# Stick-breaking attention logits as two 64-row matmuls, with norms issued earlier and a tenth weight slot

## The chip, the cores and the metric

The kernel runs on all 8 NeuronCores of one Trainium2 chip. Each core works alone on two of the sixteen sequences, with the whole weights. The metric is the device time of the slowest core in microseconds (us). The median of three runs of the kernel before is 2912.78 us (2911.24 to 2913.79).

## The reference

A trunk of two layers over x (16 sequences, 2048 positions, 1024 channels), float32. Every layer is: RMS norm, a token mixer, an output projection added to the residual h, RMS norm, and a squared-ReLU MLP with 4096 hidden channels, again added to h. A final RMS norm closes it. All norms divide by sqrt(mean(h*h) + 1e-6) over the channels.

- Layer 0 projects to 2048 columns. 512 of them go through a pooling mixer (trailing mean over 2, 4, 8 or 16 positions minus the token, then a 128x128 map); the others are a gated convolution, B * conv3(C * x).
- Layer 1 projects to 2560 columns: u and v (gelu, v layer-normed and mixed within chunks of 128 positions by a causal matrix, then multiplied with u), and q, k, v of 8 heads with 64 channels each.
- Attention has no softmax. With z = q.k/8 for a head, query t and key s < t, the weight is sigmoid(z_ts) times the product over s < j < t of (1 - sigmoid(z_tj)). Its output is the weighted sum of the v of that head.

```python
z = jnp.einsum('bhqd,bhkd->bhqk', qb, kb) * scale        # 64 channels are contracted for each head
weights = where(mask, exp(log_sigmoid(z) + suffix), 0.0)
out = jnp.einsum('bhqk,bhkd->bhqd', weights, vb)
```

## The kernel before, in words

**Stages.** Channels lie on the partitions, positions along the free axis. A unit is half a sequence: 1024 positions in two tiles t = 0, 1 of 512. Twelve stages follow one another on TensorE: F (all of layer 0 for a unit), M (the input projection of layer 1 and the gating), S (the output projection and the MLP of layer 1, then the final norm). The order is F M F M S F M F M S S S, over units (sequence, half) 00 00 01 01 00 10 10 11 11 01 10 11. A join below is the passage from one stage to the next.

**Matmuls.** A group is 8 (or 16) matmuls of 128x128 by 128x512 into one of three PSUM banks (`group`, L704), all issued by the helper at L626. Each uses one weight block of 128x1024 bf16 in the ring (9 slots). The ring is filled in the order of `block_order`: from float32 weights through a GpSimd DMA the first time, and from a bf16 copy afterwards. A group is followed by its evacuation, which works on ScalarE, VectorE and GpSimd.

**Norms.** The squares of h are summed in pairs (L724, L727, L752) down to four tiles; four matmuls with ones (`ps<-X,cbs` or `ps<-ffB,cbs`, at L626) sum them over partitions; ScalarE takes Ln (L776) and Exp (L781); VectorE writes eight scaled chunks (L802 into X for the next layer, L822 as output). `norm_h` runs one such norm for a tile t. An MLP ends (`mlp`) with the output blocks c = 4 to 7, first all four for t = 0 and then all four for t = 1; eight ring slots are taken at once for it.

**Residual.** After the norm that ends an F stage each chunk of h has been spilled (`hsp<-h`) and is then reloaded for the next F or S stage by `free_h` (`h<-hsp` or `h<-xT`). `out_proj` (L1216) adds the projection to h in `evac_x` at L844.

**Attention.** It runs beside the other stages, as small items between groups (`att_item`, L1408): 320 items in all, each for 128 queries, two heads and up to 512 keys. An item is two logits matmuls (L1423), a sigmoid on ScalarE (L614, in PSUM), two scans on VectorE (L1442), a difference on GpSimd (L1456) and a transposing DMA (L1465). For four items there are 8 matmuls with V (L1479) which write 64 columns of the array each, one head into each half of PSUM. The two heads of a pair have their channels on partitions 0-63 and 64-127 of qT and kT. The logits matmuls contract all 128 rows: `spread_q` (L1398) has ScalarE copy the queries into the tile `qz` (L1404), in which the other head's rows are zero.

**Order.** The order on every engine is fixed when the program is built. A planner (`Sched`, `Machine`) holds a set of fibers, each with one pending instruction, and always emits the one that could start first by its estimated durations, shifted by a bias; conditions (`yield lambda: ...`) hold a fiber back at planning time. On the chip each engine follows its list and waits only for semaphores. A change of `mode` is priced at 0.1 us when it leaves 0 and 0.21 us otherwise.

Of the kernel before, what the change touches and what calls it, by code (L numbers as in the profile page):

```python
# [7 lines left out]
BF16 = mybir.dt.bfloat16  # L8
# [11 lines left out]
RING = 9  # L20
# [352 lines left out]
B_L0IN, B_L0OUT, B_MLP, B_V, B_U, B_VV, B_K, B_Q, B_L1OUT = 0, 16, (24, 116), 88, 92, 96, 100, 104, 108  # L373
# [3 lines left out]
def _prep_weights(inp):  # L377
# [22 lines left out]
    blocks.extend(_mov(w, 512))  # L400
    for g in range(4):
        blocks.append(_blk(w, g * 128))
    blocks.extend(_mov(w, 2048))
# [43 lines left out]
class Builder:  # L447
# [32 lines left out]
    def alloc(self):  # L480
# [35 lines left out]
        self.qz = sb("qz", [128, 1, 2, 512], BF16)  # L516
# [53 lines left out]
        self.Lqz = lst("qz", 1)  # L570
        self.Lqz0 = LT("const")
        self.p_qz = Pool(range(1))
# [59 lines left out]
    def block_order(self):  # L632
# [4 lines left out]
        for kind, s, u in self.stages:  # L637
# [4 lines left out]
            elif kind == "M":  # L642
                seq(B_V, 20)
            else:
                seq(B_L1OUT, 8)
                seq(B_MLP[1], 64)
# [57 lines left out]
    def group(self, pairs, reads, evac, fine=None):  # L704
# [4 lines left out]
        self.room += n * self.rate  # L709
        if fine is None:  # L710
            yield self.mm(self.bank(bk), pairs, reads, [self.Lbank[bk]])
        else:
            for i in range(n):
                yield self.mm(self.bank(bk), [pairs[i]], reads + [fine[i]], [self.Lbank[bk]], i == 0, i == n - 1)
# [48 lines left out]
    def rms(self, x, t, ev, power, parts=((0, 4),), bias=-0.05, slack=0.0):  # L763
# [17 lines left out]
        q = Req("act", lambda e: e.activation(out=m, in_=m, func=AF.Exp, scale=power), [], [self.Lms[ms]], 0.65)  # L781
# [55 lines left out]
    def evac_x(self, c, t, ev, gcol):  # L837
# [5 lines left out]
        def evac(bk):  # L843
            yield Req("dve", lambda e: e.tensor_tensor(out=self.h[:, c, ts], in0=self.bank(bk), in1=self.h[:, c, ts],  # L844
# [75 lines left out]
    def start_x(self):  # L920
# [9 lines left out]
        for t in range(2):  # L930
            ts = slice(t * TT, (t + 1) * TT)
            self.hcount[("F", 0, 0, t)] = 8
# [22 lines left out]
    def load_h_chunk(self, nx, c, t, cond):  # L955
# [8 lines left out]
        self.hcount[k] = self.hcount.get(k, 0) + 1  # L964
# [12 lines left out]
    def mlp(self, l, ev, then):  # L977
# [36 lines left out]
        for q in range(2):  # L1014
            if q == 0:
                yield lambda: not self.finbusy
                self.rate = 1.0
                sl = yield from self.take(8)
                for t in range(2):
                    for j in range(8):  # L1020
                        yield from w1(sl[j], j, t, j == 0)
# [7 lines left out]
            n = 8 if q == 0 else 4  # L1029
# [6 lines left out]
            if q == 1:  # L1036
                self.rate = RATE_OUT
                sl = yield from self.take(8)
                for t in range(2):
                    for c in range(4, 8):  # L1040
                        yield from w2(sl[2 * c - 8:2 * c - 6], c, t, q)
                        if t == 1:
                            self.release(sl[2 * c - 8])
                            self.release(sl[2 * c - 7])
# [50 lines left out]
    def chain_pool(self, g, t, p, seq0, tn):  # L1095
# [6 lines left out]
        def evac(bk):  # L1102
# [25 lines left out]
            if seq0:  # L1128
                yield Req("pool", lambda e: e.tensor_tensor(out=PB[:, 0:16], in0=tmp, in1=A[:, 16:32],
                                                            op=ALU.subtract),  # L1130
                          [Lt, LA], [L1], 0.2)
            b2 = yield (self.banks,)
# [11 lines left out]
    def stage_F(self, n, s, u):  # L1144
        X, LX = self.X[0], self.LX[0]
        self.mixn = [0, 0]
        self.setn = 0
# [508 lines left out]
```

How the kernel before makes its waits and increments, by code:

```python
                def body(eng):  # L192
                    for o in self.ops[engname]:
                        for d in o.waits:
                            s, v = semval(d)
                            eng.wait_ge(s, v)
                        ins = o.fn(eng)
                        if o.sig:
                            if o.dma:
                                ins.then_inc(dsem[o.chan[1]], 16)
                            else:
                                ins.then_inc(esem[engname], 1)
                    if engname == "sp":
                        for d in final_waits:
                            s, v = semval(d)
                            eng.wait_ge(s, v)
```

## Time and profile before

| | |
|---|---|
| median of 3 runs | 2912.78 us |
| profiled execution, its own time | 2921.03 us |
| span of its slowest core (core 6) | 2919.3 us |
| spans of cores 0 to 3, granted clock | 2894.6 to 2901.7 us, 0.984 to 0.985 |
| spans of cores 4 to 7, granted clock | 2912.0 to 2919.3 us, 0.977 to 0.980 |
| TensorE busy, core 6 | 2801.1 us, 96% |
| ScalarE / VectorE / GpSimd busy | 52% / 48% / 44% |
| HBM traffic | 135 GB/s over the span |

The profile is of core 6. PE is the matmul part of TensorE and PEld its weight loads; DVE is VectorE, ACT is ScalarE, POOL is GpSimd, SP is the queue that issues most DMAs. The granted clock is the share of full speed (2.4 GHz) that TensorE was given; 0.5 is its 1.2 GHz level.

### The profile page before, as it was taken

What the parts mean: (1) busy time and instruction counts of PE and PEld (TensorE: products, weight loads), DVE (VectorE), ACT (ScalarE), POOL (GpSimd) and SP (SyncE); (2) the same over time, 40 slices, a digit from 0 to 9 for tenths busy, and PEclk for the clock granted to TensorE, in tenths of its full rate; (3) what the DMA queues carried; (4) which work ended last, traced back from release to release, by engine and by line L of the source; (5) the groups of instructions that cost most, each with busy time, mean ns of one, the idle gap of its engine ahead of it and who ended that gap; (6) DMA issues with size and microseconds to landing.
All of it is one profiled execution on the core that took longest, in us unless ns stands there. A gap on an engine that the chain in (4) does not pass through costs nothing.

```text
span 2919.3 us, 43744 instructions; the slowest of 8 cores (2894.6 to 2919.3 us)
## 1 busy us (share of the span) xinstructions
PE 2801.1 (96%) x12957; PEld 1252.3 (43%) x13219; DVE 1395.3 (48%) x1706; ACT 1527.9 (52%) x2488; POOL 1286.5 (44%) x1488
## 2 busy tenths in 40 slices
PE   9999889999999999899999999999999989999998
PEld 3444334444444344344444444444444434444443
DVE  5311345454635555756656444344465665544003
ACT  3544324857338464477653475633756467545351
POOL 5432515353415666545551444340455645551113
PEclk9999999999999999999999999999999999999999
DMA  7899982445768998746775344465355485456322
GB/s 166 172 181 183 200 214 79 117 128 139 215 166 139 174 185 164 193 97 144 162 177 162 86 105 118 109 166 163 99 123 123 101 216 131 120 111 180 85 80 87
DMA packets 491478, 420.24 MB, mean 144 GB/s; under 512 B 310128, under 2 KB 334960, under 8 KB 491248
## 3 DMA queue, kind: packets, MB, share of 16 engines
q1 hardware_dynamic: 465184, 370.07, 49.7%
q0 software_dynamic: 26064, 47.36, 11.5%
q8 instruction: 113, 1.85, 0.3%
q14 instruction: 117, 0.96, 0.1%
HBM read 304.23 MB, written 89.13 MB: 135 GB/s over the span
## 4 chain that ended last, share of the span: by engine, by line
PE 88%; DMA 3%; issue 3%; DVE 2%; ACT 2%; POOL 1%; SPq 0%; DVEq 0%; ACTq 0%; POOLq 0%
PE ps L626 82%; PE ps L1423 4%; PE ps L1479 2%; DMA ring<-wblk 1%; DMA Wk<-Wq 1%; DVE vt L1269 1%; POOL ps L1116 0%; DMA stg<-xT 0%; ACT tmp L614 0%; DVE P L1442 0%; DMA oT<-stg 0%; ACT ps L614 0%; DVE X L802 0%; DVE X L752 0%; DVE h L871 0%
## 5 line engine op out<-in xcount | busy, mean ns | idle before, releaser
L626 PE MATMUL ps<-X,ring 128*128 128x512 bf16 x6016 | 1397.2, 385 | 35.1 <-DMA ring<-wblk 5.9
L626 PEld LDWEIGHTS ps<-X,ring 128*128 128x128 bf16 x6144 | 603.3, 99 | 777.9 <-issue 131.3
L1456 POOL TENSOR_TENSOR Wq<-P 128x1024 bf16<-128x1024 f32 (+2 forms) x320 | 530.2, 1659 | 590.2 <-DVE P L1442 578.9
L1442 DVE TENSOR_TENSOR_SCAN P<-ps,carry,cbs 128x512 f32<-128x512 f32 x384 | 489.1, 1279 | 381.9 <-ACT ps L614 256.8
L626 PE MATMUL ps<-mix,ring 128*128 128x512 bf16 x2752 | 654.6, 381 | 9.0 <-DMA ring<-wblk 2.8
L626 PE MATMUL ps<-ffB,ring 128*128 128x512 bf16 x2008 | 479.9, 379 | 2.1
L871 POOL TENSOR_TENSOR h<-tmp,h 128x512 f32<-128x512 f32 x220 | 287.4, 1307 | 346.1 <-DVE tmp L866 345.1
L866 DVE TENSOR_TENSOR tmp<-ps,ms 128x512 f32<-128x512 f32 x256 | 175.1, 684 | 539.4 <-PE ps L626 530.2
L614 ACT ACTIVATE tmp<-ps 128x512 f32<-128x512 f32 x512 | 303.8, 593 | 239.2 <-PE ps L626 199.0
L626 PEld LDWEIGHTS ps<-mix,ring 128*128 128x128 bf16 x2816 | 274.5, 98 | 340.8 <-issue 29.7
L614 ACT ACTIVATE ps<-ps 128x1024 f32<-128x1024 f32 (+2 forms) x320 | 280.0, 878 | 158.3 <-PE ps L1423 157.6
L626 PEld LDWEIGHTS ps<-ffB,ring 128*128 128x128 bf16 x2048 | 200.4, 98 | 241.7 <-issue 0.2
L1442 DVE TENSOR_TENSOR_SCAN P<-ps,cbs 128x128 f32<-128x128 f32 (+3 forms) x256 | 208.3, 819 | 175.9 <-ACT ps L614 129.0
L727 ACT ACTIVATE X2f<-h 128x512 f32<-128x512 f32 x128 | 80.5, 629 | 269.1 <-POOL h L871 191.8
L660 POOL DMA_DIRECT2D ring<-wblk x180 | 99.6, 555 | 233.9 <-PE ps L626 189.9
L727 ACT ACTIVATE mix<-tmp 128x512 bf16<-128x512 f32 x255 | 160.5, 630 | 30.8 <-DMA stg<-xT 5.3
L1423 PE MATMUL ps<-kT,qz 128*128 128x512 bf16 (+3 forms) x628 | 167.8, 351 | 6.8 <-DVE P L1442 5.7
L727 ACT ACTIVATE ffB<-tmp 128x512 bf16<-128x512 f32 x256 | 161.1, 629 | 24.1 <-ACT tmp L614 0.7
L844 DVE TENSOR_TENSOR h<-ps,h 128x512 f32<-128x512 f32 x128 | 88.0, 688 | 157.6 <-PE ps L626 155.2
L852 ACT ACTIVATE X<-h,cfs 128x512 bf16<-128x512 f32 x128 | 92.0, 719 | 71.5 <-DVE h L844 70.9
L626 PE MATMUL ps<-ring,X 128*128 128x512 bf16 x498 | 115.9, 388 | 10.0 <-DVE vt L1269 6.7
L752 POOL TENSOR_TENSOR ffB<-ffBf 128x512 bf16<-128x512 f32 x64 | 81.9, 1285 | 72.5 <-ACT ffBf L727 70.7
(83 smaller groups left out, 1644.2 us busy)
## 6 DMA issues: line engine op xcount, KB each, us to landing
ring<-wbf SPq DMA_DIRECT2D x540, 256.0 KB, 2.9
ring<-wblk POOLq DMA_DIRECT2D x180, 256.0 KB, 7.0
wbf<-ring SPq DMA_DIRECT2D x180, 256.0 KB, 6.3
stg<-xT SPq DMA_DIRECT2D x96, 256.0 KB, 5.0
h<-xT SPq DMA_DIRECT2D x64, 256.0 KB, 8.4
hsp<-h SPq DMA_DIRECT2D x64, 256.0 KB, 4.7
h<-hsp SPq DMA_DIRECT2D x64, 256.0 KB, 7.7
oT<-mixf SPq DMA_DIRECT2D x32, 256.0 KB, 7.4
```

The costliest lines, as they stand in the source:

```text
L614: q = Req("act", lambda e: e.activation(out=out, in_=in_, func=func, **kw), reads, writes, dur, bias=bias)
L626: ins = pe.matmul(out, lhsT=l, rhs=r, start=(first and i == 0), stop=(last and i == n - 1), skip_group_check=True)
L660: (lambda slot, b, src: lambda e: e.dma_start(out=self.ring[:, slot, :], in_=src[b]))(slot, b, src),
L727: a = Req("act", lambda e: e.activation(out=out, in_=in_, func=AF.Square), reads, writes, 0.63, bias=bias)
L752: q = Req(eng, lambda e: e.tensor_tensor(out=X[:, SQ[i][2], t * TT:(t + 1) * TT].rearrange("p (a n) -> p a n", a=2), in0=Xf[:, SQ[i][0], h ...
L844: yield Req("dve", lambda e: e.tensor_tensor(out=self.h[:, c, ts], in0=self.bank(bk), in1=self.h[:, c, ts], op=ALU.add), [], [self.Lbank[b ...
L852: yield self.any_of(d, Req("act", lambda e: e.activation(out=X[:, c, ts], in_=self.h[:, c, ts], func=AF.Copy, scale=g), [self.Lh[c][t], se ...
L866: yield Req("dve", lambda e: e.tensor_tensor(out=self.tmp[:, b, :], in0=self.bank(bk), in1=self.ms[:, r2, :], op=ALU.mult), [self.Lms[r2]] ...
L871: q = Req(eng, lambda e: e.tensor_tensor(out=self.h[:, c, ts], in0=self.tmp[:, b, :], in1=self.h[:, c, ts], op=ALU.add), [self.Ltmp[b]], [ ...
L1423: ins = pe.matmul(zt[:, h * 512:h * 512 + w], lhsT=qz[:, h, r * 128:(r + 1) * 128], rhs=self.kT[:, a, k0:k0 + w], start=True, stop=True, s ...
L1442: yield Req("dve", (lambda h: lambda e: e.tensor_tensor_scan(out=P[:, h, 0:w][:, ::-1], data0=zt[:, h * 512:h * 512 + w][:, ::-1], data1=l ...
L1456: yield Req("pool", lambda e: e.tensor_tensor(out=W4, in0=P[:, :, 1:w + 1].rearrange("p h (j n) -> p h j n", n=128), in1=P[:, :, 0:w].rear ...
```

## The change

The logits matmuls contract 64 rows each: the first head's from partitions 0-63 of qT and kT, the second's from 64-127, into two PSUM banks. The tile `qz`, its memsets and its copies go. The memory that it took becomes a tenth ring slot. The planner prices such an item as `mode=1`.

In the norms, `norm_h` of both tiles is spawned before the MLP of an F stage with a bias of -2, and the Exp gets a bias of -2. M stages begin with the four u blocks, and a first group may take its input chunk by chunk (`ok`). Blocks are taken from the ring one by one where eight or four were taken. In an F stage the wait for the final norm of the stage before (`finbusy`) moves behind three of the four groups. `hcount` becomes a set: `out_proj` no longer waits for all eight chunks of h, and `evac_x` waits for its own. The reload of h in an M stage is spread over groups 16 to 31 of that stage (`mg`).

```diff
@@ -17,7 +17,8 @@
 EPS = 1e-6
-RING = 9
+TAILC = 4
+RING = 10
 RATE_IN = 0.4
@@ -370,7 +371,7 @@
-B_L0IN, B_L0OUT, B_MLP, B_V, B_U, B_VV, B_K, B_Q, B_L1OUT = 0, 16, (24, 116), 88, 92, 96, 100, 104, 108
+B_L0IN, B_L0OUT, B_MLP, B_V, B_U, B_VV, B_K, B_Q, B_L1OUT = 0, 16, (24, 116), 92, 88, 96, 100, 104, 108
 NBLK = 180
@@ -397,9 +398,9 @@
     w = inp["cd_w_in"][0]
-    blocks.extend(_mov(w, 512))
     for g in range(4):
         blocks.append(_blk(w, g * 128))
+    blocks.extend(_mov(w, 512))
     blocks.extend(_mov(w, 2048))
@@ -513,7 +514,6 @@
         self.ao = sb("ao", [128, 2, 512], BF16)
-        self.qz = sb("qz", [128, 1, 2, 512], BF16)
         o0 = self.off
@@ -567,9 +567,6 @@
         self.Lao = lst("ao", 2)
-        self.Lqz = lst("qz", 1)
-        self.Lqz0 = LT("const")
-        self.p_qz = Pool(range(1))
         self.LCY, self.LCC = lst("cy", 3), lst("cc", 3)
@@ -640,7 +637,7 @@
             elif kind == "M":
-                seq(B_V, 20)
+                seq(B_U, 20)
             else:
@@ -701,16 +698,19 @@
-    def group(self, pairs, reads, evac, fine=None):
+    def group(self, pairs, reads, evac, fine=None, ok=None):
...
         self.room += n * self.rate
+        self.mg += self.inm
         if fine is None:
...
             for i in range(n):
+                if ok is not None:
+                    yield ok(i)
                 yield self.mm(self.bank(bk), [pairs[i]], reads + [fine[i]], [self.Lbank[bk]], i == 0, i == n - 1)
@@ -778,7 +778,7 @@
         self.banks.free(bk)
-        q = Req("act", lambda e: e.activation(out=m, in_=m, func=AF.Exp, scale=power), [], [self.Lms[ms]], 0.65)
+        q = Req("act", lambda e: e.activation(out=m, in_=m, func=AF.Exp, scale=power), [], [self.Lms[ms]], 0.65, bias=-2)
         q.tab = AF.Ln
@@ -834,13 +834,14 @@
-    def evac_x(self, c, t, ev, gcol):
+    def evac_x(self, c, t, ev, gcol, hk):
...
         def evac(bk):
+            yield lambda: c in self.hcount.get(hk, ())
             yield Req("dve", lambda e: e.tensor_tensor(out=self.h[:, c, ts], in0=self.bank(bk), in1=self.h[:, c, ts],
@@ -929,7 +930,7 @@
             ts = slice(t * TT, (t + 1) * TT)
-            self.hcount[("F", 0, 0, t)] = 8
+            self.hcount[("F", 0, 0, t)] = set(range(8))
             ev = Ev()
@@ -961,7 +962,7 @@
         k = (kind, s, u, t)
-        self.hcount[k] = self.hcount.get(k, 0) + 1
+        self.hcount.setdefault(k, set()).add(c)
@@ -1015,9 +1016,11 @@
                 self.rate = 1.0
-                sl = yield from self.take(8)
+                sl = []
                 for t in range(2):
                     for j in range(8):
+                        if t == 0:
+                            sl += yield from self.take(1)
                         yield from w1(sl[j], j, t, j == 0)
@@ -1026,7 +1029,7 @@
                 self.release(sl[0])
-            n = 8 if q == 0 else 4
+            n = 8 if q == 0 else 8 - TAILC
             for c in range(n):
@@ -1035,13 +1038,15 @@
                 self.rate = RATE_OUT
-                sl = yield from self.take(8)
+                sl = []
                 for t in range(2):
-                    for c in range(4, 8):
-                        yield from w2(sl[2 * c - 8:2 * c - 6], c, t, q)
+                    for c in range(8 - TAILC, 8):
+                        if t == 0:
+                            sl += yield from self.take(2)
+                        yield from w2(sl[2 * (c + TAILC) - 16:2 * (c + TAILC) - 14], c, t, q)
                         if t == 1:
-                            self.release(sl[2 * c - 8])
-                            self.release(sl[2 * c - 7])
+                            self.release(sl[2 * (c + TAILC) - 16])
+                            self.release(sl[2 * (c + TAILC) - 15])
             self.ffgen += 1
@@ -1129,6 +1134,7 @@
                           [Lt, LA], [L1], 0.2)
+            yield lambda: t not in self.finbusy
             b2 = yield (self.banks,)
@@ -1145,6 +1151,7 @@
         self.setn = 0
+        self.mg = 0
         yield lambda: self.vbusy == 0 and self.cdone == 2
@@ -1154,12 +1161,11 @@
             if i not in blk:
-                blk[i] = [] if n == 0 else (yield from self.take(4))
+                blk[i] = []
             sl = blk[i]
...
             seq0 = u == 0 and t == 0
-            yield lambda: t not in self.finbusy
             if i == 0:
@@ -1175,8 +1181,10 @@
             for b in (1, 2, 0, 3):
+                if b == 3:
+                    yield lambda: t not in self.finbusy
                 fine = n == 0 and i == 0 and b == 1
-                if n == 0 and t == 0:
+                if t == 0:
                     sl += yield from self.take(1)
@@ -1204,34 +1212,36 @@
             return f
-        yield from self.mlp(0, ev2, then)
-
         def dst(t):
...
                 yield from f(c, *a)
-                self.free_h(nx, c, t, lambda: (c, t) in spilled)
+                nd2.add((c, t))
+                self.free_h(nx, c, t, lambda: (c, t) in spilled and self.mg >= 16 + 1 * (t * 8 + c))
             return g
         for t in range(2):
-            self.M.spawn(self.norm_h(ev2[t], t, 16, dst(t), nd2), -0.2)
+            self.M.spawn(self.norm_h(ev2[t], t, 16, dst(t), nd2), -2)
+        yield from self.mlp(0, ev2, then)
     def out_proj(self, kind, s, u, src, Lsrc, gcol):
-        sl = yield from self.take(8)
+        sl = []
         evo = [Ev(), Ev()]
...
             ts = slice(t * TT, (t + 1) * TT)
-            yield lambda: (self.mixn[t] == 8 if kind == "F" else (s, u, t) in self.mready) and \
-                self.hcount.get((kind, s, u, t)) == 8
+            yield lambda: (self.mixn[t] == 8 if kind == "F" else (s, u, t) in self.mready)
+            hk = (kind, s, u, t)
             if t == 1:
...
             for c in range(8):
+                if t == 0:
+                    sl += yield from self.take(1)
                 yield from self.group(self.wpairs(sl[c], src, ts), [self.Lring[sl[c]]] + [Lsrc[k][t] for k in range(8)],
-                                      self.evac_x(c, t, evo[t], gcol))
+                                      self.evac_x(c, t, evo[t], gcol, hk))
                 if t == 1:
@@ -1289,13 +1299,14 @@
         self.cn = [0, 0]
+        self.inm = 1
         self.use_scratch("sgu")
...
         self.qkn = 0
-        sl = yield from self.take(8)
+        su, sl = [], []
@@ -1313,7 +1324,6 @@
             ts = slice(t * TT, (t + 1) * TT)
-            yield lambda: t in self.nd3
             Lx = [LX[k][t] for k in range(8)]
@@ -1321,10 +1331,14 @@
                     self.un[t] += 1
-                yield from self.group(self.wpairs(sl[4 + g], X, ts), [self.Lring[sl[4 + g]]] + ([] if g == 0 else Lx), evac,
-                                      fine=Lx if g == 0 else None)
+                if t == 0:
+                    su += yield from self.take(1)
+                yield from self.group(self.wpairs(su[g], X, ts), [self.Lring[su[g]]] + ([] if g == 0 else Lx), evac,
+                                      fine=Lx if g == 0 else None, ok=lambda k: lambda: (k, t) in self.nd3)
                 if t == 1:
-                    self.release(sl[4 + g])
+                    self.release(su[g])
+            if t == 0:
+                sl = yield from self.take(4)
             for n in range(4):
@@ -1355,6 +1369,7 @@
                 self.release(sl[0])
+        self.inm = 0
         self.M.spawn(self.attention(s, u), 0.4)
@@ -1368,7 +1383,7 @@
                 nch = u * 2 + tq + 1
-                st = dict(left=nch, nch=nch)
+                st = dict(left=nch)
                 prev = [None] * 4
@@ -1378,9 +1393,6 @@
         yield lambda: self.qkn == 24
-        for a in range(4):
-            for tq in range(2):
-                self.M.spawn(self.spread_q(a, tq, items), 0.0)
         tot = float(sum(x["w"] for x in items))
@@ -1395,22 +1407,10 @@
-    def spread_q(self, a, tq, items):
-
-        z = yield self.p_qz
-        ts = slice(tq * TT, (tq + 1) * TT)
-        for h in range(2):
-            hp = slice(h * 64, (h + 1) * 64)
-            yield Req("act", (lambda h, hp: lambda e: e.activation(out=self.qz[hp, z, h, :], in_=self.qT[hp, a, ts], func=AF.Copy))(h, hp),
-                      [self.LqT[a][tq], self.Lqz0], [self.Lqz[z]], 0.64)
-        mine = [x["g"]["st"] for x in items if x["g"]["a"] == a and x["g"]["tq"] == tq]
-        mine[0]["z"] = z
-
     def att_item(self, s, u, x):
...
         a, c, first, end, tq, st = G["a"], G["c"], G["first"], G["end"], G["tq"], G["st"]
-        yield lambda: "z" in st
-        qz, Lqz = self.qz[:, st["z"]], self.Lqz[st["z"]]
+        il = tq * 4 + r
         zs = yield self.zsets
@@ -1420,13 +1420,11 @@
             for h in range(2):
-                ins = pe.matmul(zt[:, h * 512:h * 512 + w], lhsT=qz[:, h, r * 128:(r + 1) * 128],
-                                rhs=self.kT[:, a, k0:k0 + w], start=True, stop=True, skip_group_check=True)
+                hp = slice(h * 64, (h + 1) * 64)
+                ins = pe.matmul(zt[:, h * 512:h * 512 + w], lhsT=self.qT[hp, a, il * 128:(il + 1) * 128],
+                                rhs=self.kT[hp, a, k0:k0 + w], start=True, stop=True, skip_group_check=True)
             return ins
-        yield Req("pe", zmm, [Lqz, self.LkT[a][c]], Lz, w / 1200.0 + 0.01, bias=-0.04, wslack=0.5)
-        st["zn"] = st.get("zn", 0) + 1
-        if st["zn"] == 4 * st["nch"]:
-            self.p_qz.free(st["z"])
+        yield Req("pe", zmm, [self.LqT[a][tq], self.LkT[a][c]], Lz, w / 2400.0 + 0.07, bias=-0.04, wslack=0.5, mode=1)
         z3 = zt[:].rearrange("p (h n) -> p h n", h=2)[:, :, 0:w]
@@ -1539,9 +1537,6 @@
         yield Req("dve", lambda e: e.memset(self.cb[:, 128:640], 0.0), [], [self.Lz0], 0.3)
-        for h in range(2):
-            yield Req("pool", (lambda h: lambda e: e.memset(self.qz[(1 - h) * 64:(2 - h) * 64, :, h, :], 0.0))(h), [],
-                      [self.Lqz0], 0.8)
         yield self.dma(self.cf[:], self.cf_d, [], [self.Lcf], "cf", kb=72.0)
@@ -1601,6 +1596,8 @@
         self.main_t = 0
+        self.inm = 0
+        self.mg = 0
         self.r2 = {}
```

## Rows read from the trace of the kernel before

**Rows 1.** The page: busy time and share of each engine.

```profile
PE 2801.1 (96%) x12957; PEld 1252.3 (43%) x13219; DVE 1395.3 (48%) x1706; ACT 1527.9 (52%) x2488; POOL 1286.5 (44%) x1488
```

**Rows 2.** Waits of PE: us in total, times, longest us.

```profile
PE ps L626 <- DVE X L752: 28.2, 11, 3.9
...
PE ps L626 <- DVE vt L1269: 6.7, 8, 1.2
```

**Rows 3.** Stretches at the joins: length, PE busy (matmuls), clock, DMA share, GB/s.

```profile
353.00:371.00 18.00, 10.93 (x41) 0.76 1.04 216
786.00:804.00 18.00, 13.52 (x51) 0.91 0.90 252
1541.00:1559.00 18.00, 14.69 (x52) 0.81 0.92 258
1963.00:1981.00 18.00, 13.20 (x46) 0.81 0.79 224
...
1162.00:1202.00 40.00, 28.66 (x118) 0.87 0.87 217
2337.00:2369.00 32.00, 23.34 (x95) 0.87 1.11 247
2640.00:2669.00 29.00, 24.23 (x96) 0.88 1.02 289
```

**Rows 4.** Timeline of PE at an F to M join: start, us, instructions.

```profile
787.85 1.03 PE L626 MATMUL ps<-X,cbs 128*128 128x512 bf16 x4
791.34 1.02 PE L626 MATMUL ps<-X,cbs 128*128 128x512 bf16 x4 [2.46 <-DVE X L752]
792.67 0.38 PE L626 MATMUL ps<-X,ring 128*128 128x512 bf16 x1 [0.30 <-DVE X L802]
...
796.64 3.53 PE L626 MATMUL ps<-X,ring 128*128 128x512 bf16 x8 [0.29 <-DVE X L802]
```

**Rows 5.** The same join, other engines in the timeline.

```profile
791.11 10.68 DVE L802 SCALAR_TENSOR_TENSOR X<-h,cfs,ms 128x512 bf16<-128x512 f32 x16
...
791.94 10.68 SPq L619 DMA_DIRECT2D h<-hsp  x16
```

**Rows 6.** Timeline at the S to F join.

```profile
1166.09 0.69 ACT L776 ACTIVATE ms<-ps,cfs 128x512 f32<-128x512 f32 x1
...
1172.84 0.63 ACT L781 ACTIVATE ms<-ms 128x512 f32<-128x512 f32 x1
...
1174.76 0.73 DVE L822 SCALAR_TENSOR_TENSOR mixf<-h,cfs,ms 128x512 f32<-128x512 f32 x1
```

**Rows 7.** Timeline at an S to S join: a reload of h.

```profile
2347.55 0.44 SPq L619 DMA_DIRECT2D h<-hsp  x1
```

**Rows 8.** PE groups of L1423 by shape: count, busy us, mean ns, idle before.

```profile
L1423 PE MATMUL ps<-kT,qz 128*128 128x512 bf16 x436 | 132.3, 385 | 6.7 <-DVE P L1442 5.7 <-issue 0.6
...
L1423 PE MATMUL ps<-kT,qz 128*128 128x384 bf16 x64 | 15.6, 326 | 0.1
L1423 PE MATMUL ps<-kT,qz 128*128 128x256 bf16 x64 | 12.5, 277 | 0.0
...
L1423 PE MATMUL ps<-kT,qz 128*128 128x128 bf16 x64 | 9.0, 223 | 0.0
```

**Rows 9.** Timeline of PE within F 01, attention bursts between groups.

```profile
738.94 0.59 PE L1423 MATMUL ps<-kT,qz 128*128 128x512 bf16 x2
739.37 1.89 PE L626 MATMUL ps<-mix,ring 128*128 128x512 bf16 x8
...
774.68 1.89 PE L626 MATMUL ps<-ffB,ring 128*128 128x512 bf16 x8
776.50 1.05 PE L1479 MATMUL ps<-Wk,V 128*64 128x512 bf16 x8
777.48 1.90 PE L626 MATMUL ps<-mix,ring 128*128 128x512 bf16 x7
```

**Rows 10.** ACT group that fills the padded tile.

```profile
L1404 ACT ACTIVATE qz<-qT 64x512 bf16<-64x512 bf16 x64 | 39.8, 622 | 31.7 <-PE ps L1423 30.1
```

## The prediction

> **What bounds the kernel now.** I read the page first. TensorE is busy 2801.1 of 2919.3 us and every other engine about half of that [rows 1], so time goes only where TensorE waits, runs at a lower clock, or streams columns that it need not. The waits of PE come next: the largest item by far is 28.2 us in 11 waits, and it is the norm matmul waiting for the last pair sum (DVE X L752) [rows 2]. All waits of that view add to some 91 us. They sit at the joins, so I made a table of the joins by stretches [rows 3]. Full-array matmuls of 512 columns follow one another every 0.216 us (739.37 plus eight of them is the next start in the timeline). Length less count times 0.216 is what a stretch loses, to waits and to the clock together; a few records can be missing, so it is rather an upper value. The four F to M joins, in order: 18 - 41 x 0.216 = 9.1, then 7.0, 6.8 and 8.1 us, together 31.0. The S to F join loses 40 - 118 x 0.216 = 14.5, and the two S to S joins 11.5 and 8.3, together 34.3. The mean clock in these stretches is 0.76 to 0.91: after each wait TensorE is granted its 1.2 GHz level for a few microseconds, and the next matmuls take double.
>
> **Early norms, u blocks first, first group by chunks.** At the F to M join at 787 us the norm matmuls of t = 0 are the first thing PE does after the last output group, at 787.85 [rows 4], though the sums for t = 0 were complete long before: four groups of 16 matmuls for t = 1 (13.8 us) had run in between. So ScalarE and VectorE make X of t = 0 only then; VectorE writes 16 chunks in 10.68 us, 0.67 each [rows 5], and PE follows it one matmul at a time, until its first group is through at 796.86 [rows 4]. Moved into the 13.8 us, the chain of t = 0 is: evacuation and add about 2, square and pair sum 1.3, norm matmuls 0.9, Ln and Exp 1.4, eight chunks 5.3, so about 11 us. VectorE is otherwise used for about 1.4 of each 3.45 us there, which hides it. PE can then begin M at 787.71 with u groups. The old path spent 9.15 us up to 796.86 for 1.7 us of norms and 1.7 of group: 5.7 us are waits, and 1.2 GHz behind them costs about 1.5 more. What is late next is the norm of t = 1: its sums still come 3 us after the last group, as 791.34 shows [rows 4]. Eight groups of t = 0 (13.8 us) lie before its first use, but PE meets the norm matmuls in program order, and the planner has so far placed them 2.5 to 3.9 us too early. I leave 1.7 us per join for that: 31.0 - 4 x 1.7 = 24 us gained. Bounds: 0 (the waits only move) and 31. The gating phase behind it keeps its waits for VectorE (vt L1269, 6.7 us in 8 waits [rows 2]); eight chunks of X for t = 1 fall into it as before.
>
> **Exp with a bias, finbusy behind three groups.** In the S to F join Ln ended at 1166.78 and its Exp began only at 1172.84, with other work and table loads between them; the first output chunk started at 1174.76 [rows 6]. With the bias that is up to 6 us sooner. F may also start its first three groups (5.2 us) before the final norm is out, which covers the 3.9 us wait, the longest in [rows 2], and with it the fall to 1.2 GHz. Of 14.5 us I take 9, with bounds 0 and 14.5. The waits for chains of the convolution and pooling behind it remain.
>
> **hcount by chunk, out_proj one block at a time.** In an S to S join the projection could start during the wait for the norm of t = 1. But h of the new stage is still being reloaded as the final norm gives chunks free, at 2347.55 for one of them [rows 7], and with three PSUM banks PE gets at most three groups ahead of it; the norm needs a bank too. Of 19.8 us I take 4, bounds -6 (the banks are held and the norm is later) and 19.8.
>
> **Spread reload, tenth slot, single takes.** Sixteen loads of h were issued in 10.68 us right at the join [rows 5], where the DMA share is 0.79 to 1.04 [rows 3]. Moved behind group 16 they fall beside value and key groups, which read nothing of h, and have over 20 groups (35 us) before `out_proj`. A gain only where PE waits for ring blocks, mainly in the first join: nothing taken beyond the 24, bounds -2 and 5. Nothing else of the ring is on the path.
>
> **Logits over 64 rows.** 640 matmuls: 448 of 512 columns and 64 each of 384, 256 and 128 (640 in all, of which [rows 8] have 628 recorded) are 278,528 columns, 116.1 us at 2.4 GHz, and 0.0025 us each on top. If two halves stream together, half goes: 58.8 us. That they may is seen only in the sibling, L1479: eight matmuls of 512 columns, each on half of the columns of the array, take 777.48 - 776.50 = 0.98 us [rows 9], where one after the other would be 1.73. But there PE also pays for changing: the group before it (774.68 plus 8 x 0.216 = 776.41) ends 0.09 before the burst begins, and of the 0.98 us four pairs explain 0.86, so about 0.1 goes at each end. The padded logits pay nothing of that: 738.94 to 739.37 is 0.43 for two, as full-array matmuls do [rows 9]. In the PE timeline of core 6 the logits form 305 bursts; 263 are entered from a full-array matmul and 301 left to one (the rest stand beside a burst of L1479, which has changed already). 564 changes x 0.096 = 54 us. So the item is 58.8 - 54 = 5 us gained: 20 ns won on an item of 512 columns, 140 ns lost on one of 128. Bounds of a change: 0, and the 0.17 us by which a matmul (0.385 mean, [rows 8]) outlasts its slot of 0.216 plus a weight load of about 0.1, together 0.26 us. The latter makes 147 us, a loss of 88; the former a gain of 59. I take 0.096 as the nearest row.
>
> The Trainium skill, TensorEngine Tiling (Array Packing), section Key Properties, says that changing the tiling mode, not just the tile, drains TensorE. The trace agrees for column halves with about 0.1 us at each end [rows 9]; no run here shows it yet for row halves. By the page's Theoretical Speedup table alone (2x for a dimension of at most 64) the edit would bring the 58.8 us; the drain rule takes most of it back.
>
> **Copies into qz.** 64 ScalarE copies, 39.8 us, go [rows 10]. ScalarE is at 52% and is not what PE waits for; 0 taken, bounds 0 and 4.
>
> **Sum.** 24 + 9 + 4 + 5 = 42 us against the profiled execution's 2921.03: 2879. That execution stands 8.2 us above the median of the runs shown, so in the measure of the runs 2912.8 - 42 = 2871 us.
>
> **Rivals.**
> 1. *Changes of mode cost more than they do for column halves, and decide.* With 37 us from the joins and 58.8 from the columns, the kernel gets slower once a change costs over 95.8 / 564 = 0.17 us. For it: the planner prices leaving at 0.21 and adds 0.07 to each item, 0.38 per item together; a 128-column weight load into the row half may stand open, where L1479 loads 64 columns. Against it: the same planner overprices L1479 (0.15 + 4 x 0.216 + 0.31 = 1.32, measured 1.07). At 0.20 us: 113 - 58.8 = 54 lost, 37 won, 2930 us; at 0.26 us 2964.
> 2. *The joins give nothing back.* The early norm matmuls are put in front of output groups before their sums are ready, as the S joins show already, VectorE is late in the gating phase instead, and attention with its plan prices lands elsewhere. For it: every wait in the first row of [rows 2] is a place where the plan was too early. Against it: 13.8 us of cover for t = 0. Then only the 5 us of the logits are left, less a little: 2910 us.
> 3. *Row halves change for nothing* and joins gain as forecast: 59 + 37, 2817 us. For it: the weights of a row half can be loaded without touching the other. Against it: both ends of every L1479 burst.
>
> **How the numbers follow.** Forecast (gain of 18 to 65 us) 0.60, rival 1 0.17, rival 2 0.15, rival 3 0.08. This kernel's measurement can tell about 0.2% (6 us) from no change. Faster: 0.60 + 0.08 + a third of rival 2 = 0.73. Same: half of rival 2 and a little of rival 1, 0.09. Slower: 0.18. The forecast's own range is 2848 to 2895; for 8 in 10 I go to 2838 below, where more of the 65 us at the joins comes back, and to 2924 above, which takes in rival 2 and the near part of rival 1.
>
> **What would show it.** Early norms: in the F to M stretches `ps<-X,cbs` for t = 0 stands among the `ps<-mix,ring` groups, no one-matmul rows wait for L802, and the row DVE X L752 falls from 28 to below 15 us. Exp follows Ln within 1 us. Logits: L1423 appears as 64x512 with two starts a few ns apart and the next group 0.31 us later, 0.1 us of it the change; if the next group comes 0.4 us after, rival 1 holds, and if 0.22, rival 3. DVE vt L1269 well over 10 us would speak for rival 2. The forecast is wrong if the whole count of PE's waits stays near 90 us, or if the two starts of a pair are 0.2 us apart.

## The result: 30 us faster where 42 were forecast

Median 2883.38 us against 2913.28 us before; the ratio is 0.9888 (95% interval 0.9863 to 0.9914). The forecast was 2871. On two other chips the kernel before ran at 2896 to 2898 us. As the cores of a die run at a lower granted clock in some executions, this text uses a steadier number beside each ratio: the mean span of all cores on dies whose granted clock was at least 0.985 (rounded), over all runs of a kernel. For the kernel before it is 2888.1, 2888.2 and 2888.4 us, each measured anew on one of these two chips; for the changed kernel, on one of them, 2858.9, so 29.3 less.

In the profiled execution after, TensorE is busy 2793.9 of 2881.5 us on the slowest core (core 4). The waits of PE there (us in total, times, longest):

```profile
PE ps L623 <- DVE h L845: 11.6, 7, 3.2
...
PE ps L623 <- DVE vt L1279: 8.2, 8, 1.7
PE ps L623 <- DVE X L752: 7.8, 2, 4.5
PE ps L623 <- DMA mix<-dsp: 7.8, 1, 7.8
```

The wait for the norm's sums fell from 28.2 us to 7.8 as forecast [rows 2], but two waits stand in its place: for the reload of h in the projection (DVE h L845) and, once, for the mixer outputs (mix<-dsp). Stretches of the same length at the same joins (length, PE busy and matmuls, then the other engines, clock, DMA share, GB/s):

```profile
343.00:361.00 18.00, 16.43 (x66) 6.96 (x67) 12.55 (x19) 3.77 (x6) 7.50 (x10) 0.86 1.02 194
772.00:790.00 18.00, 18.00 (x85) 8.17 (x84) 10.50 (x16) 11.39 (x16) 2.39 (x2) 1.00 0.37 117
...
1939.00:1957.00 18.00, 18.00 (x82) 7.99 (x81) 9.72 (x14) 11.20 (x16) 2.54 (x2) 0.96 0.33 109
1161.00:1201.00 40.00, 29.89 (x122) 11.33 (x121) 29.67 (x38) 17.03 (x27) 18.96 (x31) 0.87 0.97 266
2306.00:2338.00 32.00, 24.05 (x107) 9.56 (x106) 25.24 (x30) 18.80 (x29) 12.19 (x10) 0.95 1.07 245
2609.00:2638.00 29.00, 25.74 (x100) 10.49 (x99) 15.77 (x22) 16.16 (x28) 6.34 (x5) 0.85 1.00 296
```

By length less count times 0.216 the F to M stretches lose 3.7, 0, 0 and 0.3 us, where they lost 31.0 [rows 3]. (The third has 85 matmuls like the second.) The first stretch begins inside a wait of PE from 340.07 to 344.57, and 2.9 us of it lie before 343: with these it loses 6.7. Three of these joins have no wait left. The S joins lose 13.6, 8.9 and 7.4 where they lost 34.3 in all: 4.4 gained, where 9 + 4 = 13 were forecast. The timeline of PE at the join which [rows 4] show before:

```profile
774.31 7.07 PE L623 MATMUL ps<-X,ring 128*128 128x512 bf16 x32
781.22 1.03 PE L623 MATMUL ps<-X,cbs 128*128 128x512 bf16 x4
782.08 7.07 PE L623 MATMUL ps<-ring,X 128*128 128x512 bf16 x32
```

The u groups start straight after the last output group, and the norm of t = 1 comes after four of them. The logits by shape (count, busy us, mean ns), and a pair in the timeline:

```profile
L1424 PE MATMUL ps<-kT,qT 64*128 64x512 bf16 x448 | 87.4, 389 | 4.4 <-DVE P L1440 4.4
...
L1424 PE MATMUL ps<-kT,qT 64*128 64x128 bf16 x64 | 7.4, 227 | 0.0
```

```profile
2303.44 1.89 PE L623 MATMUL ps<-ffB,ring 128*128 128x512 bf16 x8
2305.26 0.39 PE L1424 MATMUL ps<-kT,qT 64*128 64x512 bf16 x2
2305.58 5.35 PE L623 MATMUL ps<-X,ring 128*128 128x512 bf16 x24
```

Eight matmuls after 2303.44 end at 2305.17, so 0.09 us are lost on entering. The two logits matmuls and the way out take 0.32 us. In [rows 9] the padded pair took 0.43 and no more. Busy time of the logits, all four shapes, fell from 169 us [rows 8] to 114.5, but busy time leaves out the changes of mode.

### The profile page after: what moved, and what is told of

It reads as the page before. It is cut to its first block, busy times and chain, and to the rows that moved or that the text cites. A ratio compares the mean times of both kernels' runs of the same rounds, so it can differ in the third digit from the quotient of the medians.

```text
span 2881.5 us, 43787 instructions; the slowest of 8 cores (2851.7 to 2881.5 us)
## 1 busy us (share of the span) xinstructions
PE 2793.9 (97%) x13215; PEld 1197.7 (42%) x13215; DVE 1390.7 (48%) x1704; ACT 1481.5 (51%) x2418; POOL 1287.4 (45%) x1488
## 3 DMA queue, kind: packets, MB, share of 16 engines
q0 software_dynamic: 26064, 47.36, 11.6%
## 4 chain that ended last, share of the span: by engine, by line
PE 83%; DMA 6%; DVE 3%; POOL 3%; issue 3%; SPq 1%; ACT 1%; DVEq 0%; POOLq 0%; ACTq 0%
PE ps L623 79%; PE ps L1424 3%; PE ps L1477 2%; DVE P L1440 2%; DMA ring<-wblk 1%; DMA stg<-xT 1%; POOL Wq L1454 1%; SPq L616 1%; POOL h L872 1%; DMA Wk<-Wq 1%; DMA h<-xT 1%; POOL ps L1121 1%; DMA h<-hsp 1%; DVE vt L1279 1%; DMA mix<-dsp 1%
## 5 line engine op out<-in xcount | busy, mean ns | idle before, releaser
L623 PEld LDWEIGHTS ps<-X,ring 128*128 128x128 bf16 x6144 | 586.9, 98 | 769.6 <-issue 125.0
L623 PE MATMUL ps<-mix,ring 128*128 128x512 bf16 x2816 | 662.0, 382 | 12.3 <-DMA mix<-dsp 7.8
L623 PEld LDWEIGHTS ps<-mix,ring 128*128 128x128 bf16 x2816 | 265.5, 98 | 348.2 <-issue 52.4
L845 DVE TENSOR_TENSOR h<-ps,h 128x512 f32<-128x512 f32 x128 | 87.7, 686 | 133.0 <-PE ps L623 125.3
L1424 PE MATMUL ps<-kT,qT 64*128 64x512 bf16 (+3 forms) x640 | 113.2, 356 | 9.4 <-DVE P L1440 9.3
L752 POOL TENSOR_TENSOR ffB<-ffBf 128x512 bf16<-128x512 f32 x64 | 81.0, 1271 | 85.1 <-ACT ffBf L727 83.2
```

The lines of the kernel that those rows point to most:

```text
L623: ins = pe.matmul(out, lhsT=l, rhs=r, start=(first and i == 0), stop=(last and i == n - 1), skip_group_check=True)
L752: q = Req(eng, lambda e: e.tensor_tensor(out=X[:, SQ[i][2], t * TT:(t + 1) * TT].rearrange("p (a n) -> p a n", a=2), in0=Xf[:, SQ[i][0], h ...
L1424: ins = pe.matmul(zt[:, h * 512:h * 512 + w], lhsT=self.qT[hp, a, il * 128:(il + 1) * 128], rhs=self.kT[hp, a, k0:k0 + w], start=True, sto ...
```

## The experiments

The changed kernel again and eleven variants, each timed beside the kernel before. "Mean" is the number defined above. "Waits" is the sum of all distances between starts of PE that exceed 0.75 us, less 0.216 each, on the mean core: the average over the eight cores of the profiled execution. "1.2 GHz" is half the time in which PE streamed at that level, again on the mean core.

| kernel | ratio to before | mean, us | waits | 1.2 GHz |
|---|---|---|---|---|
| before | 1 | 2888.2 | 82.3 | 20.3 |
| changed, again | 0.9903 (0.9870-0.9937) | 2858.9 | 69.2 | 11.4 |
| e1 joins, padded logits | 0.9911 (0.9878-0.9944) | 2858.1 | 63.5 | 12.0 |
| e2 64-row logits alone | 1.0050 (1.0004-1.0095) | 2887.9 | 85.5 | 25.4 |
| e9 as e1, same order, 64 rows | 0.9897 (0.9841-0.9954) | 2859.3 | 70.0 | 12.8 |
| e3 nine slots | 0.9923 (0.9892-0.9955) | 2861.7 | 67.7 | 15.5 |
| e5 late norms | 0.9943 (0.9920-0.9966) | 2872.1 | 73.3 | 17.1 |
| e8 reload not spread | 0.9942 (0.9916-0.9968) | 2869.2 | 75.1 | 17.7 |
| e7 wait for all of h | 0.9915 (0.9884-0.9946) | 2862.8 | 69.7 | 14.3 |
| e6 Exp without bias | 0.9895 (0.9859-0.9930) | 2860.5 | 71.1 | 10.2 |
| e4 measured prices | 0.9916 (0.9890-0.9942) | 2860.8 | 70.7 | 16.8 |
| e10 padded price | 0.9845 (0.9786-0.9903) | 2849.8 | 62.1 | 13.0 |
| e11 e10, early reload | 0.9878 (0.9838-0.9918) | 2849.8 | 62.1 | 11.3 |

The scatter from die to die gives each mean a standard error of 0.4 to 2.0 us. So a difference below 3 us between two of these kernels is not resolved. Variants e1 to e4 ran on one chip, the others and the changed kernel on another; the kernel before gives 2888.1 and 2888.2 us there. The waits and the 1.2 GHz cost of the kernel before are from the first chip.

**The changed kernel again** (no edit).

> The changed kernel itself, as the yardstick for the kernels of this comparison. Its trace waits 71 us on the mean core and lost 15 us at the 1.2 GHz level when it was first taken; the same is expected here, and a ratio to before of 0.989 to 0.993.

As expected: 69.2 us of waits against 70.8 the first time. The 1.2 GHz level cost 11.4 us against 15.2.

**e1: joins with the padded logits.**

```diff
-lhsT=self.qT[hp, a, il * 128:(il + 1) * 128], rhs=self.kT[hp, a, k0:k0 + w]
+lhsT=qz[:, h, r * 128:(r + 1) * 128], rhs=self.kT[:, a, k0:k0 + w]
...
-RING = 10
+RING = 9
```

> The changed kernel with the joins as they are, but logits over the zero-padded query tile again, as before the change (ScalarE copies included), and nine ring slots. Theory A (a change between full array and row halves costs about 0.1 us at each end, so the logits edit is worth some 5 us; the joins carry the rest): 2888 us against 2883, at most 2893; no step of 0.1 us around L1424 pairs, two logits matmuls of 512 columns take 0.43 us again. Rival B (the 64-row logits also draw less current, and the fall of the time at 13/16 of the clock, 158 to 200 us before and 67 to 69 us after on cores 4 to 7, is theirs): the 13/16 time on cores 4 to 7 is back at 150 us or more and the time is 2900 or more. Rival C (the padded tile is as good or better when the joins are right): 2878 or less.

2858.1: within 1 us of the changed kernel, so neither theory A's 5 us nor a gain of rival C's size. The joins carry the whole gain that shows; the logits edit, the tenth slot and the copies together add nothing that does. No core of the profiled execution had any time at a granted clock of 13/16 (0.81), a third level that the records show beside full speed and 0.5; that is no verdict on rival B, since the changed kernel had none either when it was run again.

**e2: the logits edit alone**, on the kernel before.

> The kernel before with one part of the change: logits over 64 rows, priced as in the change, without the padded tile; nine ring slots, joins as before. Theory A: about 5 us faster than before, 2908 (2902 to 2914), with 0.1 us at each end of a pair. Rival B (less current): 2895 or less, with the 13/16 time on cores 4 to 7 under 100 us. Rival C (the plan prices of the items shift attention so that more waits arise): slower than before by 5 us or more.

2887.9 against 2888.1: nothing, where theory A expected 5 us. Rival B falls: two cores of the profiled execution spent 161 us each at 13/16, as the kernel before does at times. The stream of matmuls got 5 us shorter than in the profile before, of which the logits with their changes are about 2, and the cost of the 1.2 GHz level, most of it behind the joins, grew by 5 us (25.4 against 20.3).

**e9: the same order, only the operands differ.** The instruction lists of e1 and e9 are equal on all five engines.

```diff
 # e1, with spread_q, qz and its prices kept
-lhsT=qz[:, h, r * 128:(r + 1) * 128], rhs=self.kT[:, a, k0:k0 + w]
+lhsT=self.qT[hp, a, il * 128:(il + 1) * 128], rhs=self.kT[hp, a, k0:k0 + w]
```

> The joins kernel with the padded tile, planned exactly so (the same instructions in the same order on every engine, the copies into qz and nine ring slots included), only that the logits matmuls read qT and kT over 64 rows. So it is the price of the 64-row form alone. Theory A (0.1 us at each end, two halves at once): the logits take 1 to 5 us less of PE than padded, waits and the 1.2 GHz share stay at the padded kernel's 64 and 12 us, ratio to before 0.990, within 4 us of the padded kernel. Rival (the form itself disturbs: weights of a half array load in the open, or the clock falls more often because half of the rows work): the time at 1.2 GHz is above 18 us or waits are above 70, and the ratio is that of the changed kernel or worse.

With waits over 0.75 us counted as one slot of 0.216, the logits with their changes take 119.7 us of the mean core in e9 and 122.1 in e1: the form by itself is worth 2.4 us. The whole differs by 1.2 the other way, within the noise, with waits of 70.0 against 63.5 us in the same order, on different chips; so two profiled executions can differ by 6 us in their waits with no cause in the order. The 1.2 GHz level costs 12.8 us against 12.0, so the rival's clock part falls; its limit of 70 us for the waits was met only by that noise.

**e3: nine slots.**

```diff
-RING = 10
+RING = 9
```

> The changed kernel with nine ring slots in place of ten, nothing else. Theory A (the ring is not on the path; PE waits 6.3 us for ring blocks after the change against 8.7 before): within 4 us of 2883. Rival: the tenth slot carries a part of the gain in the first pass over the weights, then 2888 to 2895 and PE waits for DMA ring<-wblk of 12 us or more.

2861.7, 2.8 us slower. The time is inside theory A's 4 us, and just inside the noise. But PE waits 13 to 17 us for `ring<-wblk` on four of the eight cores (0, 1, 3, 5), as the rival said, against 4 to 9 in the changed kernel. The tenth slot is worth a little at most, and it is the padded tile's memory.

**e5: late norms.**

```diff
-        for t in range(2):
-            self.M.spawn(self.norm_h(ev2[t], t, 16, dst(t), nd2), -2)
         yield from self.mlp(0, ev2, then)
+        for t in range(2):
+            self.M.spawn(self.norm_h(ev2[t], t, 16, dst(t), nd2), -0.2)
```

> The changed kernel with the norms of an F stage spawned after its MLP with the old bias, as before the change; all other parts stay. Theory A (early norms take 24 us at the four F to M joins): 18 to 28 us slower than the changed kernel, with ps<-X,cbs for t = 0 behind the last output group again and one-matmul rows that wait for X L802. Rival (the wait only moves into the gating phase): slower by less than 8 us.

2872.1, 13.2 us slower: below the 18 to 28 of theory A, far above the 8 of the rival. Its join (timeline of PE) is again as before, one matmul behind each chunk:

```profile
772.72 0.59 PE L623 MATMUL ps<-X,ring 128*128 128x512 bf16 x1 [2.51 <-DVE X L802]
...
777.30 0.38 PE L623 MATMUL ps<-X,ring 128*128 128x512 bf16 x1 [0.29 <-DVE X L802]
```

Where the early norms gain and where they lose shows on the mean core, as waits plus the 1.2 GHz cost (an F to M join here is the 46 us before the first gating matmul of the M stage, the stage behind it lasts to 15 us after the last one, and the M 01 to S 00 join is the 55 us after that):

| place | before | changed, again | e5 | e8 |
|---|---|---|---|---|
| first F to M join | 10.1 | 5.3 | 6.8 | 10.3 |
| M stage behind it | 8.8 | 1.8 | 1.9 | 11.0 |
| other three F to M joins | 14.8 | 0 | 14.6 | 2.8 |
| M 01 to S 00 join | 0 | 9.1 | 2.8 | 0 |

In three joins, undoing the early norms brings back all that was lost there before; in the first they are worth 1.5 us; and 6.3 us go again at the M 01 to S 00 join, where the wait for the mixer outputs is 2.4 us in e5 and 7.3 in the changed kernel. That an M stage which starts earlier reaches these loads before they have landed is the explanation that fits; no run moves the loads alone.

**e8: the reload not spread.**

```diff
-self.free_h(nx, c, t, lambda: (c, t) in spilled and self.mg >= 16 + 1 * (t * 8 + c))
+self.free_h(nx, c, t, lambda: (c, t) in spilled)
```

> The changed kernel without the spread of the h reload: each chunk is reloaded as soon as it is normed and spilled. Theory A (a new wait of 7 to 9 us at the join from M 01 to S 00 comes from the spread: 16 reloads of h run just when the mixer outputs are loaded, with the float32 weights of the first pass beside them): that wait falls from 7.8 to 3 us or less, and the kernel is 0 to 6 us faster than the changed one. Rival (the wait comes from the shorter M stage alone): the wait stays at 7 us or more.

The wait for mix<-dsp is gone, as theory A said, but the kernel is 10.3 us slower, not faster. At the first F to M join the eight reloads for t = 0 are now issued among the output groups, and the float32 blocks that PE needs next are late (timeline of SP and of PE, core 1):

```profile
338.99 7.20 SPq L616 DMA_DIRECT2D h<-xT  x8
...
360.80 8.75 PE L623 MATMUL ps<-ring,X 128*128 128x512 bf16 x32 [6.12 <-DMA ring<-wblk]
```

Between 335 and 362 us on core 4 such a block took 14.4 us from issue to landing, in the changed kernel 8.3 (`--dma` of both runs):

```profile
ring<-wblk POOLq DMA_DIRECT2D x8, 256.0 KB, 14.4
```

The first join and the M stage behind it wait 15.7 us on the mean core in e8, 6.0 in the changed kernel. By releaser, small waits included, the wait for `ring<-wblk` rose by 3.9 us (4.9 against 1.0), and the gating phase's wait for VectorE by 5.6 (vt L1279 and vn L1265, 7.7 against 2.1). So the late blocks are shown, but they are less than half of it. This is the step that the prediction counted at nothing.

**e7: all eight chunks of h awaited.**

```diff
             hk = (kind, s, u, t)
+            yield lambda: len(self.hcount.get(hk, ())) == 8
```

> The changed kernel, but the output projection waits again (when planned) until all eight chunks of h for its tile have their reload issued, as before the change. Theory A (in an S stage PE only gets three groups ahead of the reload of h, so going by chunk is worth little): within 3 us of the changed kernel; the waits for DVE h L845 (11.6 us) fall and a wait for the norm (X L752) of about as much returns. Rival (by chunk is worth the 4 us taken in the prediction or more): 4 us slower or more.

3.9 us slower: the 4 us of the prediction, not the "within 3" of the expectation. The two S to S joins lose 20.6 us on the mean core, waits and 1.2 GHz cost together, against 15.9. DVE h L845 leaves the longest waits, X L752 is at 14.5 on the slowest core (11.4 in the changed kernel again).

**e6: Exp without its bias.**

```diff
-[], [self.Lms[ms]], 0.65, bias=-2)
+[], [self.Lms[ms]], 0.65)
```

> The changed kernel without the bias of -2 on the Exp of a norm. Theory A (the Exp used to come up to 6 us after its Ln, and the norm at the S to F join with it): the S1 to F join (11.7 us of waits in the changed kernel) grows by 3 to 6 us, the whole is 4 to 8 us slower than the changed kernel. Rival: another engine hides it and the time stays within 3 us.

1.6 us slower, within the rival's 3 and within the noise. Around the S to F join (from 35 us before the first pooling matmul to 30 behind it) the mean core waits 11.5 us against 10.7, not the 3 to 6 more of theory A.

**e4 and e10: the planner's prices.** e4 sets each change to 0.1 us, the pair to `w / 2400.0 + 0.01` and the burst with V to 0.03 on top of its columns. e10 (the end of the line):

```diff
-w / 2400.0 + 0.07, bias=-0.04, wslack=0.5, mode=1)
+w / 1200.0 + 0.01, bias=-0.04, wslack=0.5)
```

> The changed kernel, with the planner's prices set to what the trace shows: 0.1 us for each change of mode (0.1 and 0.21 before), 0.01 us on top of the columns for a logits pair (0.07 before), 0.03 for the burst with V (0.15 before). Nothing of the computation changes, only the order. Theory A (the plan runs late by 0.2 us per item, 70 us in the whole, so that PE comes to evacuations too early): PE's waits fall from 74 to 60 us or less and the time to 2872. Rival (the plan's slack on PE does not matter, the joins are planned by other engines' times): within 5 us of 2883.

> The changed kernel (64 rows, no padded tile, ten ring slots), but the planner prices a logits pair as it priced the padded one: columns / 1200 plus 0.01 us, no change of mode. Theory A (what the changed kernel lost against the joins with padded logits comes from the plan: with 0.38 us on each item the plan runs up to 0.2 us late per item): waits of 66 us or less on the mean core and 5 to 12 us faster than the changed kernel. Rival (the plan's price does not matter, each order has its own luck at the joins): waits of 68 to 75 us and within 4 us of the changed kernel.

e4 is 1.9 us slower, which is noise, e10 9.1 us faster than the changed kernel, which is not. True prices bring nothing, so my reason for the gain of e10 (a plan that runs late) does not hold. The waits of e10 are 7 us fewer, 4.4 of them in the middle of S 00 (3.0 against 7.4). Whether that is a property of the price or the luck of one order, these runs don't tell.

**e11: e10 with the reload over groups 2 to 17.**

```diff
-self.mg >= 16 + 1 * (t * 8 + c)
+self.mg >= 2 + 1 * (t * 8 + c)
```

> A version that might beat both: 64 rows, ten slots, the logits pair priced as columns / 1200 plus 0.01 us without change of mode, and the reload of h spread over groups 2 to 17 of an M stage in place of 16 to 31. Theory A: the loads are over before the mixer outputs are loaded, so the 7.3 us wait at the join from M 01 to S 00 goes to 3 us or less and the kernel gains 3 to 6 us over the one with that price alone (2849.8 us on the mean undisturbed core). Rival: the early loads hold up the norm of t = 1 or the ring, and it is within 2 us of that or slower.

The wait for mix<-dsp is gone (0 against 7.3 us), and the first M stage waits 7.4 us instead of 1.8: nothing gained, as the rival said, but not for its reason. On all eight cores the M stage waits for VectorE's gating work, not for a DMA (PE ps L1273 <- DVE vn L1265, 5.2 to 6.2 us; before the change 4.6 on the mean core). Before it, in the join, the wait for `ring<-wblk` is 1.9 us against 1.0. With e8 this shows that the mixer wait needs the reloads beside it. What their earlier place costs is a wait for VectorE, and why VectorE is later there stays open.

## Why the prediction was right in direction and too large

**Logits: right mechanism, 5 us forecast, 2 measured.** The two starts of a pair lie 3 ns apart in the timeline, so the halves stream together. Entering costs 0.096 us more than a full-array follower; leaving costs 0.103, not 0.096. With 271 entries and 302 exits in the timeline of core 0 that is 57.1 us against the 58.8 saved: 1.7 us, and 2.4 between e1 and e9. Neither is resolved in the time of the kernel. Rival 1 (0.17 us and more) and rival 3 (nothing) are out.

The Trainium skill (TensorEngine Tiling (Array Packing), Key Properties) says that a change of tiling mode drains TensorE. For row halves the trace now agrees, with about 0.1 us at each end; the page's 2x (Theoretical Speedup) holds for the stream alone.

**Early norms: right in the joins, too large in the whole.** I took 24 us for the early norms, the u blocks first and the first group by chunks together. The four joins gave just that: 31.0 went to 4.0, or to 7.0 with the part of the wait before 343. But the term stands in the sum as if nothing behind the joins would change, and there it was mis-sized: undoing the norms alone (e5) costs only 13.2. No run undoes the u blocks or the chunks; with late norms (e5) they leave three joins at 14.6 us of 14.8, so by themselves they bring nothing there. Two things take the difference. PE meets the norm of t = 0 too early in the first join, among the output groups (timeline of PE, core 4):

```profile
344.57 1.86 PE L623 MATMUL ps<-X,cbs 128*128 128x512 bf16 x4 [4.50 <-DVE X L752]
```

This is rival 2's mechanism, in one join of four. (Rival 2's other sign, the row of vt in the gating phase well over 10 us, did not come: 8.2.) And behind M 01 stands a new wait, for the mixer outputs. PE asks for them 17 us after the issue of the first (833.05), where it was 20 before (851.95 to 872.24). There the changed kernel issues one load in 5.1 us, with five reloads of h and the float32 blocks in the same stretch; the dsp loads take 14.2 us to land in the median (12.1 before), and PE waits 7.8 us. The queue of SP, and the issues between 826 and 858 us with their time to landing:

```profile
833.05 5.11 SPq L616 DMA_DIRECT2D mix<-dsp  x1
```

```profile
ring<-wblk POOLq DMA_DIRECT2D x8, 256.0 KB, 9.3
...
mix<-dsp SPq DMA_DIRECT2D x8, 128.0 KB, 14.2
```

Both are needed for it: later norms (e5) bring the wait from 7.3 to 2.4 us on the mean core, reloads elsewhere (e8, e11) to 0.

**Exp and finbusy: 9 us forecast, 1 to 4 us gained.** Exp does follow Ln at once, at 1170.13 where Ln began at 1169.35 and took 0.69; before, 6.1 us lay between them [rows 6]. F starts before the final norm is out. But PE then waits for the evacuation of a gated convolution, `mix L1091` (timeline of PE and of VectorE at the S to F join):

```profile
1178.67 0.69 DVE L1130 SCALAR_TENSOR_TENSOR pb<-ps,pa 128x512 bf16<-128x512 f32 x1 [2.80 <-POOL rtmp L1127]
...
1179.94 0.68 DVE L1091 TENSOR_TENSOR mix<-ps,cy 128x512 bf16<-128x512 f32 x1
...
1180.77 3.35 PE L623 MATMUL ps<-X,ring 128*128 128x512 bf16 x8 [4.25 <-DVE mix L1091]
```

A wait of 3.9 us went and one of 4.3 came: 14.5 us lost became 13.6 on the slowest cores. On the mean core, between the bounds given for e6, waits and 1.2 GHz cost went from 17.4 to 13.7 (14.4 in the first profile). The new wait is not for what `finbusy` guards. Its group had ended by 1176.5, but VectorE first stood 2.8 us before the pooling's `pb`, for GpSimd, and wrote one output chunk; only then came L1091. That order is the plan's; no run changes it. The bias by itself is not resolved (e6).

**By chunk: 4 us forecast, 3.9 measured** (e7), with the cause that both texts name: PE now waits for h L845 (11.6 us) where it waited for the norm.

**Spread reload and slot: 0 forecast, 10.3 and 2.8 measured** (e8, e3; the latter within the noise). The prediction's bound of 5 was wrong. It saw the DMA share of 1.04 at the first join [rows 3] but put no price on it. With early norms eight loads of 256 KB stand before the float32 blocks that PE needs next, and the gating phase behind them is later too (e8). The latter part, the larger, is seen but not explained.

Two readings in the prediction are slightly off and change nothing: the waits of PE in that view add to 93 us, not 91, and M could begin at 787.85 [rows 4], not 787.71.

**The sum.** Undoing one part at a time gives 13.2 + 10.3 + 3.9 + 2.8 + 1.6 = 31.8, and the logits 0 to 2, against 29.3 for the whole. That the parts add up so nearly is no proof that they are independent: the mixer wait needs two of them. The u blocks first, the first group by chunks, the single takes and the moved `finbusy` were not undone. By account, from before to the changed kernel again, the mean core's waits fell by 13.1 us, the cost of the 1.2 GHz level by 8.9, and the remaining stream by 3.7 (the single-matmul gaps of 0.3 us and the logits). That the total lies inside the forecast's range is in part luck: the reload, counted at 0, made up for much of what was missed elsewhere.

## What to carry to other kernels

Measure the price of changing the array's mode on a burst that is already there, and count the changes: at 0.2 us per visit a pair of 512 columns, which saves 0.21, just pays, and by the same sum anything narrower loses. When a join is closed, ask what the next stage then reaches sooner, and read the DMA rows of that place: transfers that were moved out of one join can meet PE in the next. When a condition is moved back, look at the order of the engines behind it: the next wait may be for one that stands in line behind a slower engine.

## What was not expected of the hardware

A wait of PE is not always followed by the same stretch at 1.2 GHz. In the changed kernel's second profile the wait of 4.4 us at the S to F join was followed by 3.4 us of it on core 1 and 6.8 on the seven others, and a few waits of 3.1 to 3.7 us by none. That, and waits that themselves differ (62 to 82 us in the first profile), put equal orders on eight cores up to 30 us apart (2851.7 to 2881.5 us). A second thing adds to it. In the profile before, cores 4 to 7 spent 158 to 202 us at a granted clock of 13/16 and cores 0 to 3 61 us; after, cores 4 to 7 spent 67 to 69. On another chip the changed kernel spent none, and e2 and e8 had it on two cores each (161 and 152 us). As an estimate, 3/16 of that time is lost: 11 us for 61, up to 38 for 202. So much of a difference between single profiled executions can be due to it.
